# State-space products of an S5 layer as four strips of 32 columns of the PE array

## The chip, the core and the metric

The kernel runs on one core of one Trainium2 chip. Its engines work side by side, each with its own list of instructions, and meet at semaphores: TensorE (PE) multiplies, VectorE (DVE) and ACT (ScalarE) do elementwise work and read the matmul results from PSUM banks, POOL (GpSimd) does elementwise work in SBUF, and DMA queues move data. A matmul has two instructions on TensorE: LDWEIGHTS, which puts the stationary operand (here up to 128x128) into the array, and MATMUL, which streams the moving operand past it. The metric is the device time of one execution in microseconds, the median of several runs.

## The reference

A two-layer encoder trunk on 512 tokens of width 1024. Layer 0 is a feed-forward half, an S5 state-space mixer with a gated output (GLU), and another feed-forward half. Layer 1 has latent attention in the place of the mixer. The change touches the mixer alone:

```python
def s5_mixer(h, ...):            # 64 groups of 16 channels, 64 complex states each
    u = h.reshape(bsz, seq, S5_GROUPS, S5_GROUP)
    lam_bar = exp(lam * step);  b_bar = ((lam_bar - 1) / lam)[..., None] * b
    bu = b_bar @ u               # per group, complex
    states: x_t = lam_bar * x_{t-1} + bu_t
    y = Re(C x) + d_skip * h
    z = gelu(y) @ w_glu
    return z[..., :D_MODEL] * sigmoid(z[..., D_MODEL:])
```

## The kernel before

The kernel keeps the residual stream in SBUF, 8 tiles of 128 features by 512 tokens. Nearly all of its time goes to the large products of the feed-forward parts, the GLU and the attention. Each of those is three matmuls of 128x512 in a reduced fp32 type (lines 1614 to 1616), because weights and activations are split in a high and a low part.

The state-space stage lies at about 405 to 455 us of the span. It takes T = 8 tokens as one step, so that a sequence of 512 tokens has 64 steps. In one step a group has 8 x 16 = 128 inputs, 128 outputs and 2 x 64 = 128 real state numbers. All three maps between them are then matrices of 128x128 per group, multiplied with 64 columns (the steps):

- `step_input(k)`, line 1791: inputs to what the step adds to the states (matrix `O_B`), into bank k % 2
- `from_inputs(k)`, line 1801: inputs to outputs within the step (matrix `O_T`), into bank 4 + k % 2
- `from_states(k)`, line 1808: states at the start of the step to outputs (matrix `O_C`), added to the same bank

The 64 groups are worked on in 8 blocks of GB = 8. A bank holds 8 groups of 64 columns side by side. The matrices of a block were made earlier, stored to DRAM and are loaded to one of six slots (`op_slot`). The products are in plain fp32, and the trace records two passes (a load and a matmul each) for one such product.

Between `step_input` and `from_states` other engines work on a whole block at once, 128x512: ACT copies the input (L912) and swaps its two halves of 64 partitions in PSUM (L916, L917), POOL and DVE multiply with a cosine and a sine table (L664, L1381) and add (L1383), DVE runs the recurrence over the steps as one scan (L1388), ACT swaps the halves of the result (L916, L917), and POOL and DVE turn it back (L664, L1396, L1401), which gives `state`. After `from_states` ACT applies the GELU (L934). The output then goes through DRAM to get back into its token layout, and is split in high and low parts for the GLU.

The order of the work is written out by hand, each engine in its own function. On TensorE the step inputs run three blocks ahead of the states and the products from inputs two blocks ahead. `keep_warm` (L1644) issues products of ones by ones whose result nobody reads, where TensorE would otherwise be idle. The semaphores that TensorE waits for are `s_un` (scaled inputs), `s_slot` (matrices loaded), `s_js` (the bank of the step input was read), `s_y` (the output bank was read) and `s_xs` (the state is ready).

Of the kernel before, what the change touches and what calls it, by code (L numbers as in the profile page):

```python
# [32 lines left out]
P = 128  # L33
# [12 lines left out]
STEPS = SEQ // T  # L46
GB = 8
# [60 lines left out]
O_B, O_COS, O_SIN, O_C, O_T = 0, 1024, 1536, 2048, 3072  # L108
OPS = 4096


def build(nc, xT, wstream, cols, consts, mask, pos, lam, bcd, dskip, out):
# [7 lines left out]
    def at(name, shape, dt, offset):  # L120
        return nc.alloc_sbuf_tensor_at(name, shape, dt, offset=base + offset)
# [61 lines left out]
    UY = at("u_and_y", [P, GROUPS, STEPS], F32, o_h + 16 * K)  # L183
# [4 lines left out]
    XS = at("state", [P, 2, GB, STEPS + 1], F32, o_5)  # L188
# [22 lines left out]
    BK = [nc.alloc_psum_tensor(f"bank{i}", [P, SEQ], F32) for i in range(8)]  # L211
# [81 lines left out]
    def half_bank(q):  # L293

        return out_bank(FFN1B, DT - 1) if q == 0 else in_banks(BASE[FFN1B], 1)[1]
# [28 lines left out]
    def op_slot(k):  # L324
        return SLOT[k % N_SLOTS][:]
# [91 lines left out]
    with nc.Block() as block:  # L417
# [1191 lines left out]
        def _(pe):  # L1609
            mm = nc.tensor.matmul  # L1610

            def three(bank, hi, lo, x_hi, x_lo, start, cols=None):

                mm(bank, hi, x_hi, start=start, stop=True, skip_group_check=True)  # L1614
                mm(bank, hi, x_lo, start=False, stop=True, skip_group_check=True)  # L1615
                return mm(bank, lo, x_hi, start=False, stop=True, skip_group_check=True)  # L1616

            def tile(c, k):

                r = c % RING  # L1620
                return W[:, r, 0, k * P:(k + 1) * P], W[:, r, 1, k * P:(k + 1) * P]
# [152 lines left out]
            pe.wait_ge(s_sq, SQ_OF[N_S5] + DT)  # L1774
            mm(total[:], ONES[:], SQ[:, (DT - 1) % 2, :], start=False, stop=True, skip_group_check=True).then_inc(s_ssq, 1)

            def group(ap, g, n=P):
                return ap[:, g * n:(g + 1) * n]

            def step_input(k):  # L1780
                ops = op_slot(k)
                if k == 0:
                    pe.wait_ge(s_un0, 1)
                else:
                    pe.wait_ge(s_un, k)
                pe.wait_ge(s_slot[k], 16)
                if k >= 2:

                    pe.wait_ge(s_js, k - 1)
                for g in range(GB):  # L1790
                    last = mm(group(BK[k % 2], g, STEPS), group(ops[:, O_B:O_B + 1024], g), UY[:, k * GB + g, :],  # L1791
                              start=(g == 0), stop=True, skip_group_check=True)
                last.then_inc(s_s, 1)

            def from_inputs(k):
                ops = op_slot(k)
                if k >= 2:

                    pe.wait_ge(s_y, k - 1)
                for g in range(GB):  # L1800
                    mm(group(BK[4 + k % 2], g, STEPS), group(ops[:, O_T:OPS], g), UY[:, k * GB + g, :],  # L1801
                       start=(g == 0), stop=True, skip_group_check=True)

            def from_states(k):
                ops = op_slot(k)
                pe.wait_ge(s_xs, k + 1)
                for g in range(GB):
                    last = mm(group(BK[4 + k % 2], g, STEPS), group(ops[:, O_C:O_T], g), XS[:, k % 2, g, 0:STEPS],  # L1808
                              start=False, stop=True, skip_group_check=True)
                last.then_inc(s_yp, 1)  # L1810

            keep_warm(4, BK[7])
            pe.wait_ge(s_zero, 1)
            step_input(0)
            step_input(1)
            from_inputs(0)
            step_input(2)
            keep_warm(1, BK[5])
            from_inputs(1)
            for k in range(BLOCKS):  # L1820
                from_states(k)
                if k + 3 < BLOCKS:
                    step_input(k + 3)
                elif k < BLOCKS - 1:

                    pe.wait_ge(s_js, BLOCKS)
                    keep_warm(1, BK[0])
                if k + 2 < BLOCKS:
                    from_inputs(k + 2)
# [11 lines left out]
            for q in range(2):  # L1841
                pack(KVD + q)
                for k in range(DT):
                    if q == 0:
                        pe.wait_ge(s_h_lo, H_BASE[KVD] + k + 1)
                    last = three(BK[4 + q][:], *tile(KVD + q, k), H[:, k, 0, :], H[:, k, 1, :], k == 0)
# [27 lines left out]
            for q in range(2):  # L1874
                pack(DQ + q)
                for k in range(DT):
                    if q == 0:
                        pe.wait_ge(s_h_lo, H_BASE[DQ] + k + 1)
                    last = three(BK[q][:], *tile(DQ + q, k), H[:, k, 0, :], H[:, k, 1, :], k == 0)
# [18 lines left out]
            for t in range(4):  # L1898
                last = mm(sums[:, t:t + 1], SQ[:, 1, t * P:(t + 1) * P], ONES[:, 0:1], start=(t == 0), stop=True,
                          skip_group_check=True)  # L1900
# [82 lines left out]
            for k in range(DT):  # L1983
                last = three(BK[DT - 1][:], *tile(WO + DT - 1, k), H[:, k, 0, :], H[:, k, 1, :], k == 0)
# [27 lines left out]
            for q, side in enumerate(HALVES):  # L2012
                for f in range(FT):
# [3 lines left out]
                    last = three(half_bank(q)[:, side], *tile(first + at, part), G[:, f, 0, side], G[:, f, 1, side], f == 0)  # L2017
                    if q == 1 and f == 0:
                        pe.wait_ge(s_sum, ADDED[N_FINAL])
                        for t in range(4):  # L2020
                            mm(total[:, t:t + 1], ACC[:, t * P:(t + 1) * P], ONES[:, 0:1], start=(t == 0), stop=True,
                               skip_group_check=True)
# [115 lines left out]
```

## Time and profile before

| | |
|---|---|
| three runs | 1801.22, 1801.21, 1799.46 us; median 1801.21 |
| profiled execution | 1800.29 us, of which the span is 1798.5 us |
| granted TensorE clock, mean | 0.998 |
| TensorE busy | 1779.8 us, 99% |
| weight loads busy | 1459.5 us, 81% |
| VectorE / ACT / POOL busy | 931.6 / 641.4 / 306.9 us |
| from the first state-space product to the first GLU product | 408.69 to 454.32, 45.63 us |

The profile is of one execution. Busy time counts from an instruction's start to its recorded end. Matmuls overlap in the array and their ends are modelled, so the distance between the starts of matmuls, or the length of a piece in the chain of waits, tells their rate, and the mean duration of one doesn't. PEld is the row of weight loads, which overlap the matmuls. The chain of waits follows the work that ended last back from the end, at each step to what released it.

### The profile page before, as it was taken

To read this page: it belongs to the slowest core of one execution; us is meant where nothing else is said; L and a number is where in the kernel's file an instruction comes from. 1 tells how busy PE (TensorE), PEld (TensorE's weight loads), DVE (VectorE), ACT (ScalarE), POOL (GpSimd) and SP (SyncE) were. 2 spreads that over 40 slices of the span, in tenths; PEclk is the share of its full clock that TensorE was granted. 3 is DMA by queue.
4 is the path that set the end of the run, shared out by engine and by line. 5 is a ranking of instruction groups with operands and counts; after the bars stand their busy time and mean duration, and the time that the engine had idled before them with its cause. 6 is when DMAs were issued, how large, how long until landed. Compare 5 with 4: busy or idle time off the path is not lost.

```text
span 1798.5 us, 21542 instructions
## 1 busy us (share of the span) xinstructions
PE 1779.8 (99%) x8142; PEld 1459.5 (81%) x8142; DVE 931.6 (52%) x1107; ACT 641.4 (36%) x868; POOL 306.9 (17%) x268
## 2 busy tenths in 40 slices
PE   8999999999999999999999999999999999999998
PEld 6888788889888888888888888888866788888887
DVE  7777968747555334433374344333664554444333
ACT  6232232347434333332253333222454433333222
POOL 8884615016014000000000000000100200000000
PEclk9999999999999999999999999999999999999999
DMA  5345555588422222232223222222410332322221
GB/s 195 111 153 145 159 150 148 164 302 318 135 94 96 103 94 93 97 102 94 94 82 108 102 93 93 98 101 94 123 36 1 106 105 95 103 94 93 97 91 48
DMA packets 80979, 207.25 MB, mean 115 GB/s; under 512 B 24049, under 2 KB 34417, under 8 KB 79889
## 3 DMA queue, kind: packets, MB, share of 16 engines
q1 hardware_dynamic: 69664, 189.86, 31.9%
q0 software_dynamic: 2784, 14.29, 2.3%
q10 hardware_dynamic: 8464, 2.20, 0.5%
q8 instruction: 44, 0.72, 0.2%
q14 instruction: 23, 0.18, 0.0%
HBM read 183.25 MB, written 23.07 MB: 115 GB/s over the span
## 4 chain that ended last, share of the span: by engine, by line
PE 91%; DVE 4%; ACT 2%; issue 2%; DMA 1%; SPq 1%; POOL 0%; ACTq 0%; DVEq 0%
PE bank L1614 28%; PE bank L1616 28%; PE bank L1615 28%; PE bank L1943 1%; DVE w_split L1158 1%; PE bank L1924 1%; PE bank L1926 1%; PE bank L1791 1%; PE bank L1808 1%; PE bank L1801 1%; PE bank L1686 1%; ACT w_split L748 1%; PE bank L1935 0%; DMA x_res<-xT 0%; PE bank L1644 0%
## 5 line engine op out<-in xcount | busy, mean ns | idle before, releaser
L1158 DVE TENSOR_TENSOR w_split<-w_raw,w_split 128x1024 fp32r<-128x1024 f32 x296 | 388.4, 1316 | 618.0 <-ACT w_split L748 617.2
L1614 PE MATMUL bank<-h_split,w_split 128*128 128x512 f32 x1504 | 589.5, 392 | 4.6 <-DVE w_split L1329 2.7
L1616 PE MATMUL bank<-h_split,w_split 128*128 128x512 f32 x1504 | 585.7, 389 | 0.0
L1615 PE MATMUL bank<-h_split,w_split 128*128 128x512 f32 x1504 | 585.6, 389 | 0.0
L748 ACT ACTIVATE w_split<-w_raw 128x1024 fp32r<-128x1024 f32 x296 | 311.9, 1058 | 635.8 <-PE bank L1616 626.8
L1614 PEld LDWEIGHTS bank<-h_split,w_split 128*128 128x128 f32 x1504 | 282.4, 188 | 66.3 <-DVE w_split L1329 3.2
L1615 PEld LDWEIGHTS bank<-h_split,w_split 128*128 128x128 f32 x1504 | 282.5, 188 | 59.2 <-issue 1.4
L1616 PEld LDWEIGHTS bank<-h_split,w_split 128*128 128x128 f32 x1504 | 282.4, 188 | 58.9
L1614 PE MATMUL bank<-g_split,w_split 128*128 128x512 f32 (+1 forms) x854 | 328.4, 385 | 0.1
L1616 PE MATMUL bank<-g_split,w_split 128*128 128x512 f32 (+1 forms) x854 | 327.8, 384 | 0.0
L1615 PE MATMUL bank<-g_split,w_split 128*128 128x512 f32 (+1 forms) x854 | 327.8, 384 | 0.0
L551 POOL TENSOR_TENSOR sq_sum<-sq_sum,sq 128x512 f32<-128x512 f32 x39 | 51.1, 1311 | 1063.4 <-ACT sq L767 1063.4
L1614 PEld LDWEIGHTS bank<-g_split,w_split 128*128 128x128 f32 x854 | 160.5, 188 | 31.8 <-ACT k_window L797 0.6
L1615 PEld LDWEIGHTS bank<-g_split,w_split 128*128 128x128 f32 x854 | 160.5, 188 | 31.6
L1616 PEld LDWEIGHTS bank<-g_split,w_split 128*128 128x128 f32 x854 | 160.5, 188 | 31.6
L754 ACT ACTIVATE gate<-gate 128x512 f32<-128x512 f32 x88 | 55.7, 632 | 212.0 <-DVE gate L1168 212.0
L1172 DVE TENSOR_TENSOR g_split<-gate,g_split 128x512 f32 (+1 forms) x88 | 69.8, 794 | 80.7 <-ACT g_split L756 80.7
L1170 DVE TENSOR_TENSOR gate<-gate,bank 128x512 f32<-128x512 f32 x88 | 60.6, 688 | 62.7 <-ACT gate L754 62.7
L756 ACT ACTIVATE g_split<-gate 128x512 f32 (+1 forms) x88 | 55.6, 632 | 72.7 <-DVE gate L1170 72.7
L1168 DVE TENSOR_TENSOR gate<-bank,rstd 128x512 f32<-128x512 f32 x88 | 60.1, 683 | 1.4 <-ACT rstd L785 1.4
L760 ACT ACTIVATE h_split<-x_res,cols 128x512 fp32r<-128x512 f32 x48 | 33.0, 717 | 51.0 <-DVE x_res L1284 48.2
L767 ACT ACTIVATE sq<-x_res 128x512 f32<-128x512 f32 x41 | 25.6, 623 | 50.4 <-DVE x_res L1284 38.4
(287 smaller groups left out, 1198.1 us busy)
## 6 DMA issues: line engine op xcount, KB each, us to landing
w_raw<-wstream SPq DMA_DIRECT2D x296, 512.0 KB, 3.5
op_slot<-s_ops SPq DMA_DIRECT2D x5, 2048.0 KB, 10.5
s_ops<-ops_out SPq DMA_DIRECT2D x16, 512.0 KB, 3.1
op_slot<-s_ops POOLq DMA_DIRECT2D x3, 2048.0 KB, 14.2
s_ops<-c_pow POOLq DMA_DIRECT2D x8, 512.0 KB, 5.3
s_ops<-k_window SPq DMA_DIRECT2D x64, 64.0 KB, 3.4
x_res<-xT SPq DMA_DIRECT2D x8, 256.0 KB, 7.5
s_u<-x_gained ACTq DMA_DIRECT2D x8, 256.0 KB, 5.9
```

The costliest lines, as they stand in the source:

```text
L551: nc.gpsimd.tensor_tensor(ACC[:], ACC[:], SQ[:, k % 2, :], ALU.add).then_inc(s_sum, 1)
L748: nc.scalar.activation(W[:, r, 0, :], RAW[:, r, :], ACT.Copy).then_inc(s_hi, 1)
L754: nc.scalar.activation(GT[:], GT[:], ACT.Silu).then_inc(s_silu, 1)
L756: nc.scalar.activation(gt_part(f, 0), GT[:], ACT.Copy).then_inc(s_g_hi, 1)
L760: nc.scalar.activation(dst[:, k, 0, :], X[:, k, :], ACT.Identity, scale=col(gains + k)).then_inc(s_h_hi, 1)
L1158: tt(W[:, r, 1, :], RAW[:, r, :], W[:, r, 0, :].bitcast(F32), ALU.subtract).then_inc(s_lo, 1)
L1168: tt(GT[:], gb[:], RSTD[:], ALU.mult).then_inc(s_gate, 1)
L1170: tt(GT[:], GT[:], ub[:], ALU.mult).then_inc(s_read, 1)
L1172: tt(gt_part(f, 1), GT[:], gt_part(f, 0).bitcast(F32), ALU.subtract).then_inc(s_g_lo, 1)
L1614: mm(bank, hi, x_hi, start=start, stop=True, skip_group_check=True)
L1615: mm(bank, hi, x_lo, start=False, stop=True, skip_group_check=True)
L1616: return mm(bank, lo, x_hi, start=False, stop=True, skip_group_check=True)
```

## The change

Each product of the three maps is replaced by four. Strip q takes columns 32q to 32q + 31 of the 128x128 matrix as its stationary operand, streams the same 64 columns past them, and writes partitions 32q to 32q + 31 of the same bank. `tile_position=(0, 32 * q)` places it in the columns 32q and up of the array. The waits and signals, the order of the groups and all other engines' instructions are as before: ACT still swaps the halves of the input.

```diff
-            def group(ap, g, n=P):
-                return ap[:, g * n:(g + 1) * n]
+            def strips(bank, g, ops, rhs, start):
+
+                for q in range(4):
+                    side = slice(32 * q, 32 * q + 32)
+                    last = mm(bank[side, g * STEPS:(g + 1) * STEPS], ops[:, g * P + 32 * q:g * P + 32 * q + 32], rhs,
+                              start=start, stop=True, skip_group_check=True, tile_position=(0, 32 * q))
+                return last
...
                 for g in range(GB):
-                    last = mm(group(BK[k % 2], g, STEPS), group(ops[:, O_B:O_B + 1024], g), UY[:, k * GB + g, :],
-                              start=(g == 0), stop=True, skip_group_check=True)
+                    last = strips(BK[k % 2], g, ops[:, O_B:O_B + 1024], UY[:, k * GB + g, :], g == 0)
                 last.then_inc(s_s, 1)
...
                 for g in range(GB):
-                    mm(group(BK[4 + k % 2], g, STEPS), group(ops[:, O_T:OPS], g), UY[:, k * GB + g, :],
-                       start=(g == 0), stop=True, skip_group_check=True)
+                    strips(BK[4 + k % 2], g, ops[:, O_T:OPS], UY[:, k * GB + g, :], g == 0)
...
                 for g in range(GB):
-                    last = mm(group(BK[4 + k % 2], g, STEPS), group(ops[:, O_C:O_T], g), XS[:, k % 2, g, 0:STEPS],
-                              start=False, stop=True, skip_group_check=True)
+                    last = strips(BK[4 + k % 2], g, ops[:, O_C:O_T], XS[:, k % 2, g, 0:STEPS], False)
                 last.then_inc(s_yp, 1)
```

At the start of the stage TensorE's instructions stood and stand as follows (`op_slot_92` and so on are the slots of blocks 0, 1, 2; an `x8` or `x32` counts products, not passes):

```order
 L1644 MATMUL bank<-ones 128x512 x4
-L1791 MATMUL bank<-u_and_y,op_slot_92 128x64 x8
-L1791 MATMUL bank<-u_and_y,op_slot_93 128x64 x8
-L1801 MATMUL bank<-u_and_y,op_slot_92 128x64 x8
-L1791 MATMUL bank<-u_and_y,op_slot_94 128x64 x8
+L1781 MATMUL bank<-u_and_y,op_slot_92 32x64 x32
+L1781 MATMUL bank<-u_and_y,op_slot_93 32x64 x32
+L1781 MATMUL bank<-u_and_y,op_slot_92 32x64 x32
+L1781 MATMUL bank<-u_and_y,op_slot_94 32x64 x32
 L1644 MATMUL bank<-ones 128x512
```

No group has moved; each has four times as many products of a quarter of the height, all recorded at the helper's line 1781. The same holds at the end of the stage, where the last state group is followed by the first GLU product:

```order
 L1644 MATMUL bank<-ones 128x512
-L1801 MATMUL bank<-u_and_y,op_slot_93 128x64 x8
-L1808 MATMUL bank<-state,op_slot_92 128x64 x8
+L1781 MATMUL bank<-u_and_y,op_slot_93 32x64 x32
+L1781 MATMUL bank<-state,op_slot_92 32x64 x32
 L1644 MATMUL bank<-ones 128x512
-L1808 MATMUL bank<-state,op_slot_93 128x64 x8
+L1781 MATMUL bank<-state,op_slot_93 32x64 x32
 L1614 MATMUL bank<-g_split,w_split 128x512
```

Here too only the products themselves differ; the warming products stand where they stood.

## Rows read from the trace of the kernel before

**Rows 1.** The page's first part: busy us (share of the span) and instructions of each engine.

```profile
PE 1779.8 (99%) x8142; PEld 1459.5 (81%) x8142; DVE 931.6 (52%) x1107; ACT 641.4 (36%) x868; POOL 306.9 (17%) x268
```

**Rows 2.** Chain of waits in the stage: start us, us, what; pieces in between alike.

```profile
405.34 3.43 PE bank L1644 x8
408.77 3.71 PE bank L1791 x32
412.48 1.79 PE bank L1801 x16
...
416.97 1.73 PE bank L1801 x16
418.70 1.79 PE bank L1808 x16
420.49 1.79 PE bank L1791 x16
...
441.93 1.79 PE bank L1791 x16
...
448.20 1.77 PE bank L1801 x16
449.97 1.79 PE bank L1808 x16
451.75 0.91 PE bank L1644 x2
452.67 1.84 PE bank L1808 x16
454.51 0.29 PE bank L1614
```

**Rows 3.** Timeline near 1782.7 us: start us, us, engine, line, operation, shapes.

```profile
1782.70 0.54 PEld L1998 LDWEIGHTS bank<-ones,sq 128*128 128x128 f32 x4
1782.82 0.50 PE L1998 MATMUL bank<-ones,sq 128*128 128x1 f32 x4
```

**Rows 4.** Groups with 16-column weights near 68 us: timeline, then mean ns of one.

```profile
67.67 1.64 PEld L1686 LDWEIGHTS bank<-c_pow,b_pow 128*16 128x16 f32 x16 [0.35 <-issue]
...
L1686 PEld LDWEIGHTS bank<-c_pow,b_pow 128*16 128x16 f32 x16 | 1.5, 97 | 0.5 <-issue 0.4
```

**Rows 5.** Weight loads of the stage by line: count, busy us, mean ns.

```profile
L1801 PEld LDWEIGHTS bank<-u_and_y,op_slot 128*128 128x128 f32 x128 | 15.0, 192 | 1.1 <-ACT u_and_y L934 0.6 <-issue 0.5
L1808 PEld LDWEIGHTS bank<-state,op_slot 128*128 128x128 f32 x128 | 14.9, 192 | 0.7 <-DVE state L1401 0.7
```

**Rows 6.** Windows of one block each: busy us of each engine, clock, DMA.

```profile
422.11:427.47 5.36, 5.36 (x51) 5.36 (x50) 4.22 (x6) 4.07 (x7) 3.73 (x3) 1.00 1.01 431
...
432.83:438.19 5.36, 5.36 (x51) 5.36 (x50) 3.99 (x6) 4.07 (x7) 3.74 (x3) 1.00 0.81 265
sum 16.08, PE 16.08 PEld 16.08 DVE 12.23 ACT 12.21 POOL 11.19; mean PE 5.36 PEld 5.36 DVE 4.08 ACT 4.07 POOL 3.73
```

**Rows 7.** Waits in the stage: total us, times, longest.

```profile
ACT sq L912 <- PE bank L1791: 5.8, 6, 1.2
```

**Rows 8.** Timeline at the stage's end.

```profile
451.77 0.69 DVE L1401 TENSOR_TENSOR state<-state_cos,bank 128x512 f32<-128x512 f32 x1
...
452.51 2.00 PE L1808 MATMUL bank<-state,op_slot 128*128 128x64 f32 x16
```

**Rows 9.** Chain of waits at the 16-column products.

```profile
67.74 1.85 PE bank L1686 x16
```

## The prediction

> **What bounds the kernel now.** I read the shares of the engines first, then the chain of waits, then the groups of the stage that the change touches, then that stage's windows and its waits. The page's first line shows TensorE busy for 99% of the span and VectorE for 52% [rows 1]. That row alone doesn't say that matmuls bound it, as their ends are modelled, so the chain decides. In the chain of the state-space stage every piece from 408.77 to 454.51 us is a matmul [rows 2]. The reader is to see there that a group of 16 recorded passes lasts 1.79 us wherever it stands and whatever it reads: this is a rate, not a wait. There are 24 such groups (8 blocks by three products: from inputs to step inputs, L1791; from inputs to outputs, L1801; from states to outputs, L1808). One product of 128x64 is two recorded passes, since fp32 goes through the array twice, so 8 groups of channels make 16 passes. The sum over the chain is 3.71 + 19 x 1.79 + 1.73 + 1.77 + 1.84 = 43.1 us, or 43.1/384 = 112 ns a pass. Three warming products (0.9 us each) fill the rest of the stage.
>
> What are the 112 ns? Two things happen in a pass: 128 columns of weights are loaded, and 64 columns are streamed. The warming products stream 512 columns of the same type in 3.43/8 = 0.429 us [rows 2], so 64 columns are 0.429/8 = 54 ns. The stream is therefore half of the pass, and can't be its bound. Products that move a single column behind 128 columns of weights are no quicker: their four loads take 0.54 us in all, of which one is 0.19, so (0.54 - 0.19)/3 = 117 ns lie between starts [rows 3]. The bound is the weight load. Loads of 16 columns show 97 ns and loads of 128 columns 192 [rows 4, 5]: (192 - 97)/112 = 0.85 ns a column, so 128 columns are 109 of the 112 ns, with 3 ns between two loads.
>
> The other engines have room. In a block of 5.36 us TensorE is full, VectorE has 4.08, ACT 4.07 and POOL 3.73 us [rows 6], and in the stage ACT waits for TensorE 5.8 us in six places [rows 7]. The last product group starts right behind the last state (ready at 451.77 + 0.69 = 452.46, group at 452.51) [rows 8].
>
> **The change part by part.** Every product becomes four, one for each 32 columns of the weights, each writing 32 partitions of the same bank. So 192 products become 768, and 384 passes 1536. Instruction order, waits and the other engines' work stay, as do DMAs and queues, so nothing is issued later or behind a new wait. The weight columns loaded in all stay the same (4 x 32), and the columns streamed in all become four times as many, since each strip has to see the same 64.
>
> Loads: 32 columns at 0.85 ns are 27 ns, with 3 between two loads 30. If nothing else counted, 1536 x 30 ns = 46.1 us, 3.0 more than now.
>
> Streams: 1536 passes of 64 columns. The row of 512 columns gives 54 ns for one. The 128-column passes give (1.85 us)/16 = 116 ns by the chain [rows 9] and, by their loads, (1.64 - 0.10)/15 = 103 ns [rows 4]; half of them is 52 to 58. I take 56 ns. If strips stream one after another, the load of 30 ns hides behind a stream of 56, and the stage's products take 1536 x 56 ns = 86.0 us. The term is 86.0 - 43.1 = +42.9 us.
>
> No row shows strips in different columns of the array, so the cost of one pass has to be bounded. From below: four strips load and stream entirely beside each other, 56/4 = 14 ns a pass. From above: I see no row in which passes follow each other at much less than the 112 ns of the stage, whatever their shape (103 is the least, [rows 4]), so a narrow pass could cost 112 even where both parts are short (1536 x 112 = 172.0 us, +128.9). I take 56, because the nearest rows with narrow weights (16 columns) go at the pace of their stream, with the load hidden [rows 4, 9], and a plain program of loads and streams in turn gives that. Between the ends lies a mixed case: what a strip gains beside its neighbour is limited as the two passes of one strip stand next to each other and need the same columns of the array. If only unlike strips overlap, of each two passes one hides: 768 x 56 = 43.0 us, nothing won; the serial loads (46.1) then bound.
>
> At this place the Trainium skill speaks against the change. TensorEngine Tiling (Array Packing), Instruction Overhead, says not to take the tiling factor from a dimension that is already small, as a matmul with one column lasts as long as one with about 60. The rows with one moving column agree in kind: 117 ns a pass there, 112 with 64 columns. TensorE: Matmul & The Clock Gate, Back-to-back issue gap, gives some 81 ns a matmul for a sustained stream of loads and matmuls of 128 columns; as an estimate from that page's figure, 1536 of them would be 124 us, +81. No row here shows so quick a rate.
>
> What hides it: nothing. TensorE is the chain before, in and behind the stage [rows 2], so a longer group moves the end one for one. What the longer stage gives back is small. VectorE and ACT work 4.1 us a block and would have 10.8, so every state is ready long before its group. The warming products then fill no wait, but they cost their 2.7 us as before. The last state's short wait is already covered by one of them: nothing there to save. Weight packs for the products behind the stage are split during it anyway; the one wait at its end for the last block's output (stored, loaded, split) is as long as before, as it counts from the last group. The clock is 1.00 in all windows [rows 6], 2.4 GHz, and TensorE stays busy, so I cost it at nothing; at 1.2 GHz a stream would be 107 ns, near the upper end.
>
> The sum: the profiled execution took 1800.3 us, 1798.5 of it span. 1800.3 + 42.9 = 1843.2. The median of the runs is 0.9 above the profiled one, so 1844. With 50 to 64 ns a pass the term is +33.7 to +55.2: 1835 to 1856, the forecast's own range.
>
> **The rivals.**
> Faster: strips work beside each other, loads and streams. The Trainium skill says so: TensorEngine Tiling (Array Packing), Key Properties, lets different tiles load and multiply in parallel. As a mechanism here: even if one strip's two passes (112 ns) have to follow each other, four strips side by side make a product in 112 instead of 223 ns, a group in 0.9 us. Then ACT and VectorE become the bound at about 4.1 to 4.2 us a block [rows 6]. From the first state group to the end of the last step input (418.7 to 443.7, [rows 2]) there are 4.7 blocks: 4.7 x 1.2 = 5.6 us. Before, the first state comes some 0.9 us earlier; behind the last step input the chain over ACT, the scan and the state (8.8 us now, 443.7 to 452.5) stays whole, and a part of a group's time is still seen: 0.5 lost. Gain 6, so 1795. It decides from where a strip pass costs less than 43.1/1536 = 28 ns. For it: TensorE is the only engine in the chain and half idle in its stream. Against it: serial loads alone need 30, and passes of one strip stand together.
> A little slower: strips overlap but loads don't, or passes start in order: 30 to 45 ns a pass, +3 to +26 us; at the low end 1804. For it: the load rate is the one rate that the rows show as the bound. Against it: it needs overlap that no row shows.
> Much slower: issuing a load and a matmul, or switching strips, bounds, somewhere from 64 to 112 ns. Halfway between 56 and 112 is 84 ns: 1536 x 84 = 129.0, +85.9, 1887; the end is 1930. For it: nothing in the rows goes much quicker than 103. Against it: both shapes are explained by their columns, the wide loads and the long streams.
> That the change does nothing: loads and streams overlap just so far that a strip pass costs 28 ns (26 to 30 keeps it within 0.2%).
>
> **How the numbers follow.** Forecast 0.42, a little slower 0.22, faster 0.17, much slower 0.15, nothing 0.04. A measurement of this kernel can tell about 0.2%, 3.6 us. A little slower reaches inside that bound at its low end (0.04 of its 0.22), so faster 0.18, same 0.08, slower 0.74. For 8 in 10 the range has to take in most of the faster case, so from 1794; above, it takes in the start of the much slower case, to 1872 (74 ns a pass: 113.7 us in products, +70.6).
>
> **What would show it.** Right: 1536 passes at about 56 ns between starts, groups of 64 passes lasting 3.6 us in the chain, the stage from first product to the first GLU product 88.5 us instead of 45.6, ACT and VectorE waiting over 5 us in every block, and everything behind the stage shifted by one amount. Groups under 1.8 us, with TensorE waiting for states, would be the faster case. Groups of 1.9 to 2.9 us are the little slower one. Groups of over 4.5 us, or a granted clock under 1.00 in the stage, are the much slower one. The forecast is wrong above all if the array streams unlike strips at once.

## The result and the profile after

The changed kernel took 1811.0 us (median of four runs, 1809.0 to 1813.2) against 1801.0 before: a ratio of 1.0061, 95% interval 1.0049 to 1.0073. In a repetition (e8 below) it was 1.0048 (1.0031 to 1.0064). The forecast was 1844. Slower was right, but by 10 us and not by 43, and the reason given was wrong.

First the page's shares, in the form of [rows 1]:

```profile
PE 1768.7 (98%) x9294; PEld 1443.7 (80%) x9294; DVE 932.0 (52%) x1107; ACT 641.4 (35%) x868; POOL 308.6 (17%) x268
```

There are 1152 passes more, as counted, and yet TensorE is busy 11 us *less*. The chain of waits of the kernel after, where [rows 2] had matmuls alone (start us, us, what):

```profile
405.37 3.43 PE bank L1644 x8
408.81 3.04 PE bank L1781 x190
411.84 2.00 issue
413.84 1.23 PE bank L1781 x66
...
420.41 2.00 PE bank L1781 x127
422.41 4.09 issue
426.51 3.64 PE bank L1781 x128
430.14 2.02 issue
432.16 5.56 PE bank L1781 x246
437.73 4.09 issue
...
445.55 2.23 PE bank L1781 x126
447.78 2.15 issue
449.94 2.00 PE bank L1781 x127
451.93 1.89 issue
453.82 0.35 PE bank L1781 x8
...
462.22 0.70 DVE state L1401
...
462.96 1.12 PE bank L1781 x64
464.08 0.43 PE bank L1614
```

Two things are to be seen. 190 passes take 3.04 us and 127 take 2.00, so a pass costs 16 ns, and in the steady part of the records (behind 420.41 us) eight starts follow each other in 112 ns: 14 ns each, the lower bound of the prediction. A group of 64 takes 0.9 us, half of what the full width took. And between the pieces there is "issue", time in which the engine waited for nothing that the profile shows.

The 55.3 us of this chain add up as 26.0 us of strip passes, 1.7 of warming products, 18.8 of "issue" on TensorE and 8.8 at the end. Those last 8.8 us, from 454.17 to 462.96, are the way of block 7 over ACT, VectorE's scan and back to its state. Before, the same 8.8 us lay behind the last step input too (443.7 to 452.5), but TensorE's products filled them. Now the last step input ends 10.5 us later, because of the pauses before it, and TensorE's remaining products and pauses are off the chain.

The waits put a number on it (total us, times, longest):

```profile
PEld bank L1781 <- issue: 24.5, 12, 4.3
PE bank L1781 <- issue: 20.5, 10, 4.1
...
ACT sq L912 <- PE bank L1781: 12.4, 5, 4.7
```

ACT's wait for step inputs, 5.8 us in [rows 7], has doubled. The pauses lie at 126 to 128 passes from each other or twice that (the warming products count too), and 128 passes are 256 instructions (a load and a matmul for each pass). The list of DMA queues says what 256 instructions are; first before, then after, both from 405 to 465 us (packets, MB, share of 16 engines):

```profile
q8 instruction: 4, 0.07, 0.4%
```

```profile
q8 instruction: 12, 0.20, 1.3%
```

A packet of this queue has 16 KB (0.20 MB in 12), or 256 instructions, if each has 64 bytes. The page, which counts the whole span, bears that out: 44 such packets before, 53 after, 9 more for 2304 = 9 x 256 more instructions. In the experiments below it is 3 more for 768 more instructions (e1, e4), 5 for 1280 (e7, e10) and 8 for 2048 (e9). From the first product to the GLU it is now 55.3 us (408.81 to 464.08) instead of 45.6, and that is the whole difference of the spans: 1808.3 - 1798.5 = 9.8 us.

### The profile page after: what moved, and what is told of

Its sections match the earlier page's. It is cut to its first block, busy times and chain, and to the rows that moved or that the text cites. A ratio compares the mean times of both kernels' runs of the same rounds, so it can differ in the third digit from the quotient of the medians.

```text
span 1808.3 us, 23846 instructions
## 1 busy us (share of the span) xinstructions
PE 1768.7 (98%) x9294; PEld 1443.7 (80%) x9294; DVE 932.0 (52%) x1107; ACT 641.4 (35%) x868; POOL 308.6 (17%) x268
## 4 chain that ended last, share of the span: by engine, by line
PE 89%; DVE 4%; issue 3%; ACT 2%; DMA 1%; SPq 1%; POOL 0%; ACTq 0%; DVEq 0%
PE bank L1614 28%; PE bank L1616 28%; PE bank L1615 28%; PE bank L1781 1%; PE bank L1945 1%; DVE w_split L1158 1%; PE bank L1926 1%; PE bank L1928 1%; PE bank L1686 1%; ACT w_split L748 1%; PE bank L1937 0%; DMA x_res<-xT 0%; PE bank L1644 0%; PE bank L1690 0%; DVE gate L1170 0%
```

## The experiments

Theory A: strips run beside each other in the array, and TensorE then runs out of instructions, which come 256 at a time and no quicker than one such piece in about 4 us, 6 beside heavy transfers. Theory B: the pauses belong to strips as such. All ratios are to the kernel before, measured beside it on the same chip. The experiments ran on three chips, so they are compared by these ratios.

**Two strips of 64 columns (e1_halves).**

```diff
-                for q in range(4):
-                    side = slice(32 * q, 32 * q + 32)
-                    last = mm(bank[side, g * STEPS:(g + 1) * STEPS], ops[:, g * P + 32 * q:g * P + 32 * q + 32], rhs,
-                              start=start, stop=True, skip_group_check=True, tile_position=(0, 32 * q))
+                for q in range(2):
+                    side = slice(64 * q, 64 * q + 64)
+                    last = mm(bank[side, g * STEPS:(g + 1) * STEPS], ops[:, g * P + 64 * q:g * P + 64 * q + 64], rhs,
+                              start=start, stop=True, skip_group_check=True, tile_position=(0, 64 * q))
```

> Two strips of 64 columns in the place of four of 32: half as many products (384, 768 passes, 1536 instructions on TensorE), the same columns loaded. Theory A (TensorE runs out of instructions, which are fetched 256 at a time, 2 us or, beside other transfers, 4 us a piece; strips themselves run beside each other): a group stays at about 0.9 us, but it eats only 64 instructions instead of 128, so the pauses mostly go and ACT and VectorE bound the stage; 1794 to 1798 us. Theory B (the pauses belong to strips as such, each layout change or each block draining the array): as many pauses as with four strips, over 20 us of idle time, 1808 us or more. Theory C (the two strips don't overlap, 56 ns a pass): 768 x 56 = 43 us of products, no change, 1801.

Measured: 1797.1 us, ratio 0.9983 (0.9973 to 0.9993). This beats both kernels. Its waits in the stage:

```profile
PEld bank L1781 <- DVE state L1401: 5.9, 2, 3.0
PEld bank L1781 <- ACT u_and_y L934: 5.8, 5, 2.0
...
PEld bank L1781 <- issue: 3.9, 6, 1.0
```

The waits for nothing fell from 24.5 us to 3.9, and TensorE now waits for the states and the GELU. Two passes follow each other in 58 ns, 29 each, so a group of 32 passes takes 0.93 us, the same as 64 passes of half the width. Theory A's time was hit (1794 to 1798). B fell by the waits, and C by the 29 ns a pass. The stage gained 3.3 us (the GLU starts at 451.0 instead of 454.3) and the kernel 2.4: in the middle VectorE and ACT are nearly full.

```profile
423.00:432.00 9.00, 6.86 (x211) 6.33 (x209) 8.40 (x11) 8.06 (x16) 7.88 (x7) 1.00 1.01 428
```

In these 9 us TensorE is busy for 6.86, VectorE for 8.40 and ACT for 8.06.

**Four strips, with the transfers of the last two blocks made small (e2_small_loads).**

```diff
-                sp.dma_start(op_slot(k), ops_dram[k]).then_inc(s_slot[k], 16)
+                sp.dma_start(op_slot(k)[:, 0:128], ops_dram[k][:, 0:128]).then_inc(s_slot[k], 16)
```

> Four strips of 32, but the two transfers of 2 MB that bring the matrices of blocks 6 and 7 during the stage carry 64 KB each; the last two blocks then calculate with the matrices of blocks 0 and 1. Theory A (instruction fetches that stand in line behind those transfers): the pauses of 4.1 us at 422.4 and 437.7 us shrink to about 2 us, those of 2 us stay; 4 us less than with full transfers, about 1807. Theory B (pauses belong to the strips): all pauses as they are, 1811.

Measured: 1805.1 us, ratio 1.0033 (1.0024 to 1.0043), against 1.0048 and 1.0061 with full transfers.

```profile
PEld bank L1781 <- issue: 21.1, 12, 3.7
```

The pause behind pass 826, in the transfer of block 7, was 4.3 us between starts in the change and 4.2 in its repetition, and is 1.8 here. The one behind pass 443 is less clear, 4.3 and 2.6 against 2.6. Theory A had expected both to shrink. There are as many pauses as before, so these two transfers don't make them; that a transfer lengthens a pause is clear at one place only. The time is clear of 1.0061, but its interval touches that of the repetition, 1.0048.

**The same strips, ordered by strip (e3_strip_runs).**

```diff
                 for q in range(4):
                     side = slice(32 * q, 32 * q + 32)
-                    last = mm(bank[side, g * STEPS:(g + 1) * STEPS], ops[:, g * P + 32 * q:g * P + 32 * q + 32], rhs,
-                              start=start, stop=True, skip_group_check=True, tile_position=(0, 32 * q))
+                    for g in range(GB):
+                        last = mm(bank[side, g * STEPS:(g + 1) * STEPS], ops[:, g * P + 32 * q:g * P + 32 * q + 32], rhs(g),
+                                  start=start and g == 0, stop=True, skip_group_check=True, tile_position=(0, 32 * q))
```

> Four strips of 32, the same 1536 passes, but ordered by strip: all eight groups of a block through columns 0 to 31, then all eight through 32 to 63, and so on. Theory A (unlike strips overlap, like ones can't): a group of 64 passes takes 64 x 56 ns = 3.6 us, at which pace the fetches keep up and no pause is left; stage some 88 us, 1843 to 1845. Theory B (the pauses belong to the strips or their number of instructions alone): pauses stay on top, 1860 or more. If TensorE takes matmuls out of order over the whole block, the time stays at 1811.

Measured: 1825.3 us, ratio 1.0139 (1.0119 to 1.0159); neither theory's time. The chain has no pause left:

```profile
406.78 11.51 PE bank L1782 x256
418.29 1.06 PE bank L1644 x2
419.35 48.04 PE bank L1782 x1088
```

48.04/1088 = 44 ns a pass. Within a run of one strip the starts are 56 ns apart, as forecast. At the change from one strip to the next seven of the sixteen distances are shorter: 6 and 50 ns and then five of 25 to 30. I read this as two strips at work at once, the matmuls of the next strip having been handed to the array already. That is where the 20 us to my 1845 went. With 5.6 us for 256 instructions the fetches keep up, which is what A says of the pauses. The kernel has as many strips and as many instructions as the change, at a slower pace, and no pauses on its chain: this speaks against B.

**Strips in the step inputs alone (e4_inputs_only).** The edit against the kernel before:

```diff
-                    last = mm(group(BK[k % 2], g, STEPS), group(ops[:, O_B:O_B + 1024], g), UY[:, k * GB + g, :],
-                              start=(g == 0), stop=True, skip_group_check=True)
+                    last = strips(BK[k % 2], g, ops[:, O_B:O_B + 1024], UY[:, k * GB + g, :], g == 0)
```

> Four strips of 32 in the step inputs alone (L1791 of the kernel before), the other two maps in full width. A block then has 128 + 32 + 32 = 192 instructions on TensorE instead of 96 or 384, and 0.9 + 1.79 + 1.79 = 4.5 us of work. Theory A: 192 instructions in 4.5 us ask for 256 in 6 us, which fetches of 2 to 4 us can give: few pauses, 1795 to 1798. Theory B (each change between full width and strips drains or pauses TensorE): 16 more changes of layout, 1803 or more.

Measured: 1801.6 us, ratio 1.0010 (0.9996 to 1.0025). The median is in neither theory's range (A 1795 to 1798, B from 1803). Its ten runs spread from 1795.4 to 1807.2, more than those of the other kernels, and the profiled one was one of the quick ones (1798.6):

```profile
424.78 1.79 PE bank L1815 x16
426.57 1.03 PE bank L1781 x64
427.60 1.93 PE bank L1808 x16
```

Hardly a pause is in it (1.4 us of waits for nothing, the longest 0.8). A change from full width to strips and back costs about 0.13 us each time (1.03 for 0.90, 1.93 for 1.79), 16 changes some 2 us. The longer runs had the lower mean granted clock (1.000 at 1795.4, 0.997 at 1798.6, 0.992 at 1807.2 us). What lowered it in some runs stays open, as the trace is of a quick one; so does what this kernel costs against two strips, which have as many instructions a block.

**Two strips and more warming products (e5_halves_warm).**

```diff
-            keep_warm(1, BK[5])
+            keep_warm(4, BK[5])
...
-                    keep_warm(1, BK[0])
+                    keep_warm(3 if k == BLOCKS - 2 else 1, BK[0])
```

> Two strips of 64 columns as before, and more warming products where TensorE waits for a state: four instead of one ahead of the second block's products from inputs, three instead of one ahead of the last products from states. The run with two strips showed a granted clock of 0.5 from 418.7 and again from 449.4 us, each for 3.4 us, behind waits of 3.1 and 3.3 us; six products at the start of the GLU then took 0.43 instead of 0.23 us. Theory A: the clock stays at 1.00, the last state group takes 0.9 instead of 1.5 us and the GLU's start is 1.2 us quicker: 1.5 us less than with two strips alone, about 1795.5. Rival: the clock cost is hidden, as the first GLU products wait for the last outputs anyway: no change.

Measured: 1797.6 us, ratio 0.9983 (0.9973 to 0.9993), the same as without. One of its ten executions took 6590.6 us; why isn't known, and the median hardly feels it. The windows at the GLU's start, first with two strips alone, then here:

```profile
449.80:453.10 3.30, 3.30 (x29) 2.80 (x26) 1.58 (x4) 1.86 (x3) 0.38 (x1) 0.50 1.00 260
```

```profile
450.00:455.00 5.00, 5.00 (x35) 4.10 (x30) 1.87 (x3) 1.75 (x3) 0.05 (x1) 1.00 0.89 266
```

The granted clock did stay at 1.00 through the stage. The intervals of the two ratios are 0.1% wide to each side, 1.8 us, so the times can't tell a gain of 1.5 us from none. The two traces can be compared in their parts. From the first product of the stage to the GLU it is 41.6 us instead of 42.0, and the first six GLU products take 1.5 instead of 2.5 us. Of these 1.3 us about 0.5 are lost again within the next 50 products, where TensorE now waits for outputs on their way through DRAM:

```profile
PEld bank L1614 <- DVE g_split L1408: 0.8, 2, 0.5
```

So the rival was right in part. In these two traces the low clock cost some 0.8 us, half of what the forecast had; that it cost nothing isn't shown.

**Full width with instructions that do nothing (e6_full_nops).**

```diff
+            def idle():
+                for _ in range(12):
+                    pe.nop()
```

> The kernel before, in full width, with 12 instructions that do nothing behind each of the 192 products: as many instructions on TensorE in the stage as with four strips (3072), and no strip. Theory A (TensorE runs out of instructions): long pauses at every 256 instructions although nothing in the array has changed, time above 1805. Theory B (pauses belong to strips): a product takes at most a little longer, evenly, and there are no pauses; 1800 if such instructions cost under 9 ns each.

Measured: 1801.6 us, ratio 1.0004 (0.9994 to 1.0015). The trace has 21542 instructions, as before, and the page 44 instruction packets, as before, where 2304 more instructions would be 9 more: they never reached TensorE. The run says nothing on either theory.

**TensorE swaps the halves (e7_pe_swap).**

```diff
-                swap_input(k)
...
+                    at = g * P + 64 * ((1 - q) if turned else q)
...
-                    pe.wait_ge(s_js, k - 1)
+                    pe.wait_ge(s_sc, k - 1)
+                    pe.wait_ge(s_z, k - 1)
```

> As the kernel with two strips and more warming products, and in addition TensorE itself writes the step inputs with their halves swapped, as two more strips from the other half of the matrix, so ACT's two copies in PSUM (1.14 us a block) are gone. A block has 256 instead of 192 instructions on TensorE. If TensorE has the room that the two strips gave it (3.7 of some 4.3 us a block), the chain from step input to scan is 1.2 us shorter at the stage's start and VectorE alone (4.1 to 4.2 us a block) sets the pace: 1 to 2 us less than without, about 1794. Rival: 256 instructions a block are again as many as the fetches bring in 4 us, so pauses come back and it is slower than without, 1798 or more.

Measured: 1802.1 us, ratio 1.0010 (1.0001 to 1.0020). The rival's time was right, but the trace doesn't bear out its mechanism. The chain does show long pieces of "issue":

```profile
419.41 1.28 POOL state_cos L664
420.69 3.76 issue
...
424.48 0.08 POOL input_cos L664
```

They lie between two instructions of POOL, and POOL waits there, over ACT's copy, for TensorE's step input. TensorE itself is at work all the time, and its waits for nothing are about those of the kernel with two strips and more warming products (4.2 us there):

```profile
PEld bank L1780 <- issue: 4.6, 4, 2.8
```

```profile
420.00:428.00 8.00, 8.00 (x280) 8.00 (x279) 4.40 (x6) 3.88 (x7) 4.21 (x4) 1.00 0.97 377
```

280 passes in 8.0 us are 256 instructions in 3.7 us, without a pause, beside 377 GB/s of transfers (part of them can have been in store). What the edit added is a wait: the swapped input is written to the bank that the scan of two blocks before reads (`s_z`), so the third step input has to wait for the first scan:

```profile
414.16 2.08 PE L1780 MATMUL bank<-u_and_y,op_slot 128*64 128x64 f32 x64 [1.81 <-DVE state_turned L1386]
```

It takes twice as long besides (2.0 us), and the four warming products behind it (3.7 us) no longer fit into the wait: the first state is ready at 416.9 and its group starts at 420.8. Without the edit both are at 418.2. From the first product to the GLU it is 47.1 us instead of 41.6; 3.9 of the 5.5 us are this delay, and one pause of 2.8 us with a low clock behind it (437.8 to 441.1) can account for the rest. The run doesn't show that 256 instructions a block are too many.

**The change once more (e8_change_again).**

> The changed kernel itself once more, on the same chip as the others of this call, to compare them with it directly: 1.006 of the kernel before, pauses of 2 and 4 us at the same instructions.

Measured: 1809.9 us, ratio 1.0048 (1.0031 to 1.0064). Pauses behind the same passes (190, 316, 443, 571, 826, ...), but not all of the same length: behind 316 it was 4.0 and not 2.1 us, behind 443 it was 2.6 and not 4.3. So the place is fixed by the count, and the length isn't.

**The rate by itself (e9_bursts).** Full width everywhere, no strip in the kernel.

```diff
+            def burst(bank):
+                for _ in range(256):
+                    mm(bank[0:16, 0:8], ONES[:, 0:16], ONES[:, 0:8], start=True, stop=True, skip_group_check=True)
```

> The disputed rate by itself, without a strip: the kernel before, full width everywhere, with two bursts of 256 small extra fp32 products (16 columns of weights, 8 moving columns, 512 passes, 1024 instructions on TensorE each), one just ahead of the state-space products, while the matrices of the blocks are being loaded, one ahead of the feed-forward part behind the latent key, where the DMA engines are some 20% busy. Theory A (TensorE is given at most 256 instructions in about 4 us, 6 us beside heavy transfers): each burst shows pauses of some 2 us or more, 128 passes apart, and takes 14 to 17 us in the quiet place and up to 24 in the busy one. Theory B (pauses belong to strips): both bursts run through without pauses in 8 to 12 us, at 15 to 20 ns a pass.

Measured: one run, 1841.0 us with both bursts. The chain in the busy place, then in the quiet one:

```profile
406.55 5.19 PE bank L1815 x199
411.74 2.65 issue
414.39 3.56 PE bank L1815 x128
417.95 1.27 issue
419.22 3.56 PE bank L1815 x128
422.78 3.19 issue
425.98 1.67 PE bank L1815 x57
```

```profile
936.88 7.56 PE bank L1815 x293
944.43 1.35 issue
945.79 3.58 PE bank L1815 x128
949.37 0.16 issue
949.52 2.60 PE bank L1815 x91
```

This decides against B: products without strips pause too, at every 128 passes. The times are in A's ranges (21.1 us in the busy place, 15.2 in the quiet one). Pauses of 2 us or more didn't come in the quiet place, as a pass took 25 to 27 ns and not the 15 to 20 that I had expected. The windows of the two (quiet, then busy; clock, DMA share and GB/s at the end):

```profile
936.90:952.10 15.20, 13.69 (x513) 13.48 (x512) 11.80 (x14) 4.55 (x6) 0.00 (x0) 0.67 0.14 39
408.00:428.00 20.00, 12.88 (x459) 12.64 (x456) 3.19 (x4) 3.37 (x4) 3.00 (x2) 0.54 0.79 302
```

Where 128 passes take 3.6 us, a piece of 256 instructions came 3.7 us after the one before it in the quiet place (945.79 to 949.52), and 4.8 and 6.8 us in the busy one (414.39, 419.22, 425.98). In the changed kernel the pieces begin 5.7 to 6.1 us apart while the matrices are being loaded (420.41, 426.51, 432.16), and 4.4 us apart later (445.55, 449.94). The first pause comes after 199 and 293 passes, so something is in store at the start.

**Four strips for the step inputs, two for the other maps (e10_mixed).**

```diff
-                    strips(BK[4 + k % 2], g, ops[:, O_T:OPS], UY[:, k * GB + g, :], g == 0)
+                    strips(BK[4 + k % 2], g, ops[:, O_T:OPS], UY[:, k * GB + g, :], g == 0, 2)
...
-                    last = strips(BK[4 + k % 2], g, ops[:, O_C:O_T], XS[:, k % 2, g, 0:STEPS], False)
+                    last = strips(BK[4 + k % 2], g, ops[:, O_C:O_T], XS[:, k % 2, g, 0:STEPS], False, 2)
```

> Four strips of 32 for the step inputs, two of 64 for the other two maps: 128 + 64 + 64 = 256 instructions a block on TensorE, between the 192 of two strips everywhere (0.9983) and the 384 of four (1.005 to 1.006), with 0.9 us of array time for every group as in both, and ACT's copies in place. Theory A (the number of instructions decides): time between, about 1.001, 1800 to 1803 us; pauses again every 128 passes, but shorter than with four strips. Theory B (the pauses come with strips of 32, whatever their number): about as slow per strip group as the change, a third of its loss over two strips, also about 1801; here the places of the pauses tell: under B they lie in the step inputs alone.

Measured: 1800.5 us, ratio 1.0008 (0.9998 to 1.0018), in A's range and near B's.

```profile
PEld bank L1782 <- issue: 10.1, 7, 3.9
```

The places don't decide as the expectation says. The long pauses lie behind passes 190, 443, 570 and 698, all in step inputs, where B has them. But these are the counts at which the change pauses too (190, 443, 571), and a block here has 128 passes, so every 128th falls into the same part of the block whichever theory holds. With two strips a block has 96, and there the pause behind pass 570 lies in the products from states. The count decides.

With 192, 256 and 384 instructions a block the waits for nothing are 3.9, 10.1 and 24.5 us, and the ratios 0.9983, 1.0008 and 1.0048 to 1.0061. Array time for a group is the same 0.9 us in all three. TensorE swapping the halves (e7) also has 256, at an even 29 ns a pass, and waits for nothing only 4.6 us, so it isn't the number in a block alone: the strips of 32 ask for 128 of their instructions in 0.9 us.

## Why the prediction was wrong

*The bound before.* Right. The weight load paced the passes, and TensorE was the whole chain. e3 confirms it from the other side: with 32 instead of 128 columns to load, passes in the same columns of the array went from 112 ns to the 56 of their stream.

*The streams, 1536 x 56 ns.* This step failed. "If strips stream one after another" was taken because rows with 16-column weights go at the pace of their stream, but those rows hold only products in the same columns of the array. The 56 ns were right for one strip: eight passes of the changed kernel, two of each strip, take 112 ns. What was wrong is that the four strips add up. They run side by side, loads and streams, and the term of +42.9 us measured 21.5 - 43.1 = -21.6 us of array time at full clock (1536 x 14 ns). The case was among the rivals, with its mechanism (a product in 112 instead of 223 ns, a group in 0.9 us), at 0.17. The Trainium skill's sentence that different tiles load and multiply in parallel (TensorEngine Tiling (Array Packing), Key Properties) is borne out by 14 ns a pass and 29 with two strips, and I should have given it more weight against rows that could not speak to it.

*The serial loads* (46.1 us, the rival "a little slower"). Wrong in mechanism: serial loads of 30 ns would have given 1.9 us a group, and a group took 0.9. Its range of times, +3 to +26 us, holds the result by chance.

*Nothing hides it, nothing is behind a new wait.* This failed too. It overlooked the queue that every instruction goes through. I counted "1536 passes" and never asked what they cost to deliver. Before, a piece of 256 instructions lasted 128 x 0.112 = 14 us in this stage. In the change it would last 1.8 us, and a piece takes 4 to 6 us to come. 18.8 us of the chain are such pauses, and behind them the way to the last state, 8.8 us of other engines' work, sets the end, where quicker passes gain nothing. The rival "much slower" named issuing as a bound, but as a price per instruction, paid evenly, up to 112 ns. The truth was a cheap instruction (7 ns) and a supply in lumps.

*The clock.* Costed at nothing. It did fall to 0.5 three times, each behind a pause of 2.0 or 4.1 us, for 3.4, 10.2 and 3.4 us, and 128 passes then took 3.64 us instead of 2.00. The next piece may be on its way meanwhile, so how much of that is lost is open; with two strips some 0.8 us of such a cost can be read from the traces (e5), with four its share wasn't tested.

*What would show it.* The forecast expected groups of 3.6 us at even pace. The groups of 0.9 us were those of the faster case, whose price was about 6 us gained. Two strips, with 3.9 us of waits for nothing in the stage, got 2.4 of it, so the 6 was too much in itself as well; by which term isn't shown.

## What to carry to other kernels

Small products whose time is the loading of 128 columns of weights can be split into column strips which load and stream beside each other, if neighbours in program order go to different strips. Count the instructions at the new pace: where 256 of them were used up in less than some 4 to 6 us for longer than the store lasts, TensorE waited for instructions, which the profile shows as "issue" at a fixed distance of passes. Take the widest strips that give the pace that the other engines can follow, which here were two of 64. And look for what becomes late: here it was the last step input, with 8.8 us of other engines' work behind it.

## What the runs showed of the hardware

- fp32 passes of 64 columns: 112 ns each with 128 columns of weights; 29 with two strips of 64 in turn; 14 with four of 32 in turn; 56 for one strip of 32 after itself.
- TensorE's instructions came in packets of 16 KB. Behind the first store of 200 to 290 passes, a piece of 256 came 3.7 us after another beside transfers of 39 GB/s on average over the burst, and 4.8 and 6.8 us beside some 300 GB/s. With the store, 280 passes ran through in 8.0 us beside 377 GB/s (e7).
- A small product of 16 columns of weights and 8 moving ones cost 25 ns a pass at a granted clock of 1.00 and 27 at 0.5. In the quiet place the clock was 1.00 up to 942 us and 0.5 behind it, while the burst ran from 936.88 to its first pause at 944.43: such passes back to back did not hold the clock.
- Changing between full width and strips of 32 cost about 0.13 us each way.
